# Tile 32's turn inside the pipelined rows, its next gather ahead of its scatter, and the closing norm's arguments on GpSimd

## What is computed

```
x  = x + gt1 * y
h2 = rms_norm(x) * (1 + sc2) + sh2
g  = top-1 of 4 groups, then the top-2 of its 8 experts, weights = softmax * group probability
y  = sum over the 2 experts of  w_e * ( silu(h2 @ gate_e) * (h2 @ up_e) ) @ down_e      # 1024 -> 128 -> 1024
out = rms_norm(x + gt2 * y, final_g)
```

## Time and profile before

| | us |
|---|---|
| median of 3 runs (lowest, highest) | 945.08 (943.24, 945.47) |
| the profiled execution's own time | 939.78 |
| its span in the profile | 938.0 |
| TensorE (matmul) busy | 874.8 (93%) |
| VectorE, GpSimd, ScalarE busy | 457.0, 277.3, 253.6 |
| granted TensorE clock, mean | 0.978 |

### The profile page before, as it was taken

How to read it: one execution, slowest core, us unless ns; L and a number is a source line. 1 busy time by engine, 2 the same in 40 slices (tenths; PEclk the granted TensorE clock), 3 DMA queues, 4 the chain that set the end, 5 groups by cost and what they waited for, 6 DMA issues and landing times. The chain is left out here.

```text
span 938.0 us, 17412 instructions
## 1 busy us (share of the span) xinstructions
PE 874.8 (93%) x7182; PEld 597.2 (64%) x7182; DVE 457.0 (49%) x1140; ACT 253.6 (27%) x608; POOL 277.3 (30%) x264
## 2 busy tenths in 40 slices
PE   5989999999999999999999899999999999999950
PEld 5554445565544447888887745555688888888830
DVE  4820477666731104565665324434464555555534
ACT  5320122222300102545444311221313223222203
POOL 4810000000399400524235010000023566544232
PEclk9999999999999999999999999999999999999995
DMA  9833433444101104000004037111299999998739
GB/s 343 251 94 98 152 112 112 132 148 161 29 22 46 45 1 180 3 3 3 3 3 157 5 144 304 46 78 57 101 339 313 306 305 278 276 275 252 219 57 358
DMA packets 79493, 136.33 MB, mean 145 GB/s; under 512 B 16989, under 2 KB 51002, under 8 KB 79418
## 3 DMA queue, kind: packets, MB, share of 16 engines
q1 hardware_dynamic: 69258, 118.44, 36.4%
q0 software_dynamic: 10160, 16.82, 7.5%
HBM read 123.65 MB, written 29.92 MB: 164 GB/s over the span
## 5 line engine op out<-in xcount | busy, mean ns | idle before, releaser
L752 PE MATMUL bank<-REG_W 128*128 128x512 f32 (+1 forms) x864 | 281.6, 508 | 6.5 <-DVE REG_P L1684 2.5
L752 PEld LDWEIGHTS bank<-REG_W 128*128 128x128 f32 (+1 forms) x864 | 123.3, 176 | 149.4 <-issue 144.5
L752 PE MATMUL bank<-REG_W,REG_Y 128*128 128x512 f32 x256 | 118.3, 599 | 1.4 <-DVE REG_Y L2036 1.1
L1295 ACT ACTIVATE REG_P<-bank 128x256 f32<-128x256 f32 (+2 forms) x126 | 56.9, 460 | 183.8 <-PE bank L752 149.5
L752 PE MATMUL bank<-REG_P 64*64 64x64 f32 (+1 forms) x2816 | 86.8, 222 | 7.2 <-issue 3.3
L752 PEld LDWEIGHTS bank<-REG_P 64*64 64x64 f32 x2816 | 81.1, 135 | 12.4 <-issue 5.8
L752 PEld LDWEIGHTS bank<-REG_W,REG_Y 128*128 128x128 f32 x256 | 45.6, 191 | 44.3 <-issue 44.2
L1295 ACT ACTIVATE REG_Y<-bank,mod,s 128x128 f32<-128x128 f32 x132 | 49.6, 456 | 86.5 <-PE bank L1248 86.5
L752 PEld LDWEIGHTS bank<-REG_Y,REG_W 128*128 128x128 f32 (+1 forms) x640 | 65.7, 181 | 8.4 <-issue 8.4
L752 PE MATMUL bank<-REG_Y,REG_W 128*128 128x128 f32 (+1 forms) x640 | 69.0, 276 | 2.1 <-DVE REG_Y L1905 2.1
L609 POOL TENSOR_TENSOR REG_P<-REG_P 128x1040 f32<-128x1040 f32 x2 | 4.8, 2391 | 194.8 <-DVE REG_P L1635 194.7
(11 more groups left out here) (286 smaller groups left out, 1190.9 us busy)
## 6 DMA issues: line engine op xcount, KB each, us to landing
REG_P<-in_w_ada SPq DMA_DIRECT2D x18, 1024.0 KB, 6.2
REG_W<-in_w_in SPq DMA_DIRECT2D x17, 512.0 KB
REG_P<-in_moe_w_gate SPq DMA_DIRECT2D x17, 512.0 KB, 8.3
REG_W<-in_moe_w_gate SPq DMA_DIRECT2D x16, 512.0 KB, 6.2
REG_W<-in_moe_w_up SPq DMA_DIRECT2D x16, 512.0 KB, 9.5
REG_W<-in_moe_w_down SPq DMA_DIRECT2D x16, 512.0 KB, 14.4
REG_P<-in_moe_w_up SPq DMA_DIRECT2D x14, 512.0 KB, 14.5
REG_P<-in_w_ada SPq DMA_DIRECT2D x3, 2048.0 KB, 12.1
```

The costliest lines, as they stand in the source:

```text
L752: return pe.matmul(o_, l, r, start=start, stop=stop, skip_group_check=True)
L1295: return act.activation(o_, i_, f, **kw)
```

## The change

- TensorE, ScalarE, VectorE: the condition `e + 1 < E` goes, so row 31 also transposes and modulates tile 32. In the overflow loop the transposes and the modulation move to the end of the turn and are those of the next tile (33 in the one turn here). TensorE's transposes then wait for the gather of their tile in the new places.
- GpSimd: `n_ov` is read ahead of the waits for the scatters; in the loop the next tile's gather and the signal `ov_go` stand ahead of the wait for this tile's scatter, the gather ahead of the scatter itself.
- The closing norm goes in the groups (0,1), (2,3), (4,5), (6), (7); GpSimd adds the epsilon and takes the root; VectorE only multiplies; the last tile is multiplied and written in two halves of 512 columns.

```diff
+FINAL = ((0, 1), (2, 3), (4, 5), (6,), (7,))
@@ SP
-            for j in range(NT):
+            for j in range(NT - 1):
                 sp.wait_ge(s["f_o"], j + 1)
                 sp.dma_start(outd[j * P:(j + 1) * P, :], x1[:, j]).then_inc(s_fo, 16)
+            for h in range(2):
+                sp.wait_ge(s["f_o"], NT + h)
+                sp.dma_start(outd[(NT - 1) * P:, h * 512:(h + 1) * 512], x1[:, NT - 1, h * 512:(h + 1) * 512]).then_inc(s_fo, 16)
@@ GpSimd
+            n_ov = gp.value_load(idy[0:1, 0:1], min_val=1, max_val=OVT)
             for b in range(RES):
                 gp.wait_ge(s_sc[b], 16 * len(range(b, E, RES)))
-            n_ov = gp.value_load(idy[0:1, 0:1], min_val=1, max_val=OVT)
             with gp.Fori(0, n_ov) as i:
+                gp.wait_ge(s["m_tx"], i + (E + 1))
+                gather(i + (E + 1), 0)
                 scatter_add(rows_of(i + E, 1, i + (E + 1)), 0)
+                gp.sem_inc(s["ov_go"], 1)
                 gp.wait_ge(s_sc[0], i * 16 + 16 * (len(range(0, E, RES)) + 1))
-                gather(i + (E + 1), 0)
-                gp.sem_inc(s["ov_go"], 1)
             gp.sem_inc(s["f_go"], 1)
-            for i in range(NT // 2):
+            for i, tiles in enumerate(FINAL):
+                at = slice(tiles[0], tiles[-1] + 1)
+                gp.wait_ge(s["ss_ready"], 2 * NT + tiles[-1] + 1)
+                gp.tensor_scalar(ss[:, 2, at], ss[:, 2, at], EPS, None, ALU.add).then_inc(s["f_ss"], 1)
                 gp.wait_ge(s["f_ss"], i + 1)
-                gp.tensor_tensor(rs[:, 2, at], ss[:, 2, at], mhalf[:, 0:2], ALU.pow).then_inc(s["rstd_ready"], 1)
+                gp.tensor_tensor(rs[:, 2, at], ss[:, 2, at], mhalf[:, 0:len(tiles)], ALU.pow).then_inc(s["rstd_ready"], 1)
@@ TensorE (ScalarE and VectorE in the same way)
             for e in range(1, E):
-                if e + 1 < E:
-                    ex_t(e + 1, (e + 1) % BUF, 16 * ((e + 1) // BUF + 1))
+                ex_t(e + 1, (e + 1) % BUF, 16 * ((e + 1) // BUF + 1))
                 ex_gu(e, e % 2, e % RING, ...)
                 ex_dn(e - 1, (e - 1) % 2, (e - 1) % RING, wait_free=e >= 3)
...
             with pe.Fori(0, n_ov) as i:
-                ex_t(i + E, 0, i * 16 + 16 * (E // BUF + 1))
                 ex_gu(i + E, 0, 0, "m_", s["ov_w"], i * 48 + 48, False)
                 pe.wait_ge(s["m_yd"], i + E)
                 ex_dn(i + E, 0, 0, "m_", False)
+                ex_t(i + (E + 1), 0, i * 16 + 16 * (E // BUF + 2))
@@ VectorE
-            root_args(0)
-            for i in range(NT // 2):
-                if i + 1 < NT // 2:
-                    root_args(i + 1)
+            for i, tiles in enumerate(FINAL):
                 dve.wait_ge(s["rstd_ready"], 2 * NT + i + 1)
-                for j in (2 * i, 2 * i + 1):
-                    stt(x1[:, j], x1[:, j], rs[:, 2, j:j + 1], fg, ALU.mult, ALU.mult).then_inc(s["f_o"], 1)
+                for j in tiles:
+                    wide = D if j < NT - 1 else D // 2
+                    for c0 in range(0, D, wide):
+                        stt(x1[:, j, c0:c0 + wide], x1[:, j, c0:c0 + wide], rs[:, 2, j:j + 1], fg[:, c0:c0 + wide],
+                            ALU.mult, ALU.mult).then_inc(s["f_o"], 1)
```

More of the change, by code:

```diff
@@ L520, in _ @@
                 sp.dma_start(x1[:, j], y_d[j * P:(j + 1) * P, :]).then_inc(s_w[j], 16)
-            for j in range(NT):
+            for j in range(NT - 1):
                 sp.wait_ge(s["f_o"], j + 1)
                 sp.dma_start(outd[j * P:(j + 1) * P, :], x1[:, j]).then_inc(s_fo, 16)
-            sp.wait_ge(s_fo, 16 * NT)
+            for h in range(2):
+                sp.wait_ge(s["f_o"], NT + h)
+                sp.dma_start(outd[(NT - 1) * P:, h * 512:(h + 1) * 512], x1[:, NT - 1, h * 512:(h + 1) * 512]).then_inc(s_fo, 16)
+            sp.wait_ge(s_fo, 16 * (NT + 1))
         @block.gpsimd
@@ L731, in _ @@
                     gp.sem_inc(s["ov_go"], 1)
+            n_ov = gp.value_load(idy[0:1, 0:1], min_val=1, max_val=OVT)
             for b in range(RES):
                 gp.wait_ge(s_sc[b], 16 * len(range(b, E, RES)))
-            n_ov = gp.value_load(idy[0:1, 0:1], min_val=1, max_val=OVT)
             with gp.Fori(0, n_ov) as i:
                 ch.enter(i, 4)
+                gp.wait_ge(s["m_tx"], i + (E + 1))
+                gather(i + (E + 1), 0)
                 scatter_add(rows_of(i + E, 1, i + (E + 1)), 0)
+                gp.sem_inc(s["ov_go"], 1)
                 gp.wait_ge(s_sc[0], i * 16 + 16 * (len(range(0, E, RES)) + 1))
-                gather(i + (E + 1), 0)
-                gp.sem_inc(s["ov_go"], 1)
             gp.sem_inc(s["f_go"], 1)
-            for i in range(NT // 2):
+            for i, tiles in enumerate(FINAL):
+                at = slice(tiles[0], tiles[-1] + 1)
+                gp.wait_ge(s["ss_ready"], 2 * NT + tiles[-1] + 1)
+                gp.tensor_scalar(ss[:, 2, at], ss[:, 2, at], EPS, None, ALU.add).then_inc(s["f_ss"], 1)
                 gp.wait_ge(s["f_ss"], i + 1)
-                at = slice(2 * i, 2 * i + 2)
-                gp.tensor_tensor(rs[:, 2, at], ss[:, 2, at], mhalf[:, 0:2], ALU.pow).then_inc(s["rstd_ready"], 1)
+                gp.tensor_tensor(rs[:, 2, at], ss[:, 2, at], mhalf[:, 0:len(tiles)], ALU.pow).then_inc(s["rstd_ready"], 1)
         @block.tensor
@@ L1532, in _ @@
             for e in range(E):
-                if e + 1 < E:
-                    modulated(xt[:, (e + 1) % 2], 0, e + 2, "m_tx", "m_xa", 0)
+                modulated(xt[:, (e + 1) % 2], 0, e + 2, "m_tx", "m_xa", 0)
                 hidden(e, e % 2, free=e >= 2)
@@ L1538, in _ @@
             with act.Fori(0, n_ov) as i:
-                modulated(xt[:, 0], 0, i + (E + 1), "m_tx", "m_xa", 0)
                 hidden(i + E, 0, free=False)
+                modulated(xt[:, 0], 0, i + (E + 2), "m_tx", "m_xa", 0)
             for j in range(NT):
@@ L2049, in _ @@
             for e in range(E):
-                if e + 1 < E:
-                    modulated(xt[:, (e + 1) % 2], e + 2, "m_tx", "m_xd", 1)
+                modulated(xt[:, (e + 1) % 2], e + 2, "m_tx", "m_xd", 1)
                 hidden(e, e % 2, free=e >= 2)
@@ L2061, in _ @@
                 ch.enter(i, 1)
-                modulated(xt[:, 0], i + (E + 1), "m_tx", "m_xd", 1)
                 hidden(i + E, 0, free=False)
-                dve.wait_ge(s_sc[0], 16 * len(range(0, E, RES)))
+                dve.wait_ge(s_sc[0], i * 16 + 16 * len(range(0, E, RES)))
                 result(i + E, 0)
+                modulated(xt[:, 0], i + (E + 2), "m_tx", "m_xd", 1)
             dve.wait_ge(s["xr_ld"], 16 * (NT + 1))
[L2069 to L2072, removed]
-            root_args(0)
-            for i in range(NT // 2):
-                if i + 1 < NT // 2:
-                    root_args(i + 1)
-                dve.wait_ge(s["rstd_ready"], 2 * NT + i + 1)
-                for j in (2 * i, 2 * i + 1):
-                    stt(x1[:, j], x1[:, j], rs[:, 2, j:j + 1], fg, ALU.mult, ALU.mult).then_inc(s["f_o"], 1)
+            for i, tiles in enumerate(FINAL):
+                dve.wait_ge(s["rstd_ready"], 2 * NT + i + 1)
+                for j in tiles:
[3 more added lines that the diff above has]
+                            ALU.mult, ALU.mult).then_inc(s["f_o"], 1)
 _INS = ["x", "c", "w_ada", "b_ada", "norm1_g", "norm2_g", "w_in", "w_out", "pool_w", "pool_scale", "attn_sinks", "conv_w",
```

## The result

The changed kernel takes 954.99 us (median of 6, 950.66 to 957.18) against 944.0 us before (6 runs, 940.47 to 945.47): ratio 1.0115, interval 1.0085 to 1.0145, slower by some 11 us. Forecast was +8.2 us, range +3.4 to +12.4.

A forecast was written before the change was run, and what follows sets the result against it. It took TensorE's row before 897 us, GpSimd's hand-overs to 914.44 and the 23.56 us tail as bounds. Terms +6.9 + 1.7 + 0.3 − 0.7 + 0 = +8.2 us took the 945.08 us median to 953.3, range 948.5 to 957.5.

The forecast's parts named there:

- The gather of tile 32 stops row 31: TensorE, row 31: transposes wait for a gather landing 8.0 us after issue, so gate/up starts at 896.9, not 889.94: +6.9 us.
- The clock: TensorE after its 5.7 us stop: granted clock halves for 3.4 us of work, +1.7 us, bounds 0 and 3.4.
- (a): Rival: TensorE stops at the gather but the clock stays at 2.4 GHz; +6.5 us, 951.6 us; chance 0.18.
- My row at 898: TensorE's 2.09 us gap before the overflow tile's matmuls: a short gap without a clock fall, said not to contradict the rule.
- GpSimd's hand-overs: GpSimd around the overflow tile's scatter: +0.3 us from turn 31's landing to that scatter, −0.7 us from its landing to SP's read.
- The tail: Closing norm from the first read of y_d to the end: 0 us since transfers bound it, bounds −0.6 and +1.2.
- my own last sign: Forecast is wrong if the tail from the first read of y_d differs from 23.56 us by more than 1.5 us.
- the lock: Closing norm: VectorE and GpSimd share a port pair, the loser waiting a whole instruction; VectorE's end +1.2 us, without it −2.2.
- (b): Rival: the tail also pays, +1.2 for GpSimd against VectorE and +1.0 for a delaying gather; 955.5 us; chance 0.16.
- the gather's delay: Tile 33's gather, ahead in the same queue, delays the overflow tile's scatter or the squares: charged nothing, bound +1.0 us.
- (c): Rival: tile 32's gather is there when TensorE asks, so no stop or clock loss; +0.2 us, 945.3 us; chance 0.11.
- (d): Overflow tile: pipelining gains nothing itself, its early data waiting for GpSimd; at most 1.4 us if paid in full; no separate chance.

The follow-up runs named there:

- warm22: The changed kernel with 22 extra matmul calls of unused result ahead of row 31's transposes, so TensorE works through most of its stop: ratio 1.0082 to the kernel before.
- rows_only: The changed kernel with the closing norm of the kernel before; pipelined row and GpSimd's new order stay: ratios 1.0047 and, timed again, 1.0061 to the kernel before.
- tail_only: The kernel before with only the closing norm changed, all of the change's tail: ratio 1.0033 to the kernel before.
- args_pool: The kernel before with the closing norm's arguments on GpSimd, in the four old pairs and with a whole last tile: ratio 1.0027 to the kernel before.
- order_only: The kernel before with GpSimd's new order in the overflow loop alone: ratio 0.9990 to the kernel before.
- ahead_root: The changed kernel with tile 32 gathered earlier, tile 33's gather ahead of the scatter waits, old norm with halved last tile, last pair's roots on ScalarE and VectorE: 942.38 us against 945.8.
- gather_early: The changed kernel with the overflow table loaded behind turn 26 and tile 32 gathered in GpSimd's turn 25 instead of 28: ratio 1.0031 to the kernel before.

## Why the prediction was right, and where not

- **The gather of tile 32 stops row 31, +6.9.** Right in place, cause and size: it lands 8.00 us after its issue, the idle time is 5.46 (5.7 forecast), it goes with an earlier gather (first stretch −8.1, the clock's part included) and grows with a later one. Counted without the clock, in warm22, the first stretch is 19.92 against 13.33: +6.6.
- **The clock, +1.7.** It fell as forecast. It was low for 6.8 us, and TensorE was at work for 5.0 us of them here (forecast 3.4), for 4.4, 3.6 and 3.6 in the other three profiles with the stop. The price by warm22 is 2.34 us here and 2.1 and 1.7 in the kernel of rows_only: the term was at the low end, and one execution's row couldn't size it. The fall at 70 us that I took it from lasts 3.4 us in nine of the 14 profiles and 6.8 in five. Rival (a), no fall, is out: the fall stands in all four profiles with a stop that TensorE idled through. My row at 898, the gap of 2.09 us that had no fall, was luck: in tail_only and args_pool the clock falls after that same gap of the old order (2.08 and 2.09 us), gate/up of turn 32 takes 5.35 and 5.46 us instead of 3.83, and tile 32's scatter comes 1.6 us later.
The Trainium skill (TensorE: Matmul & The Clock Gate, "Why this matters for your kernels") warns of the half clock after an idle gap between bursts of matmuls; the trace agrees (0.50 from 899.7 to 906.5).
- **GpSimd's hand-overs, +0.3 − 0.7.** Sum −1.05 measured in the changed kernel, −0.1 in order_only. From turn 31's landing (920.41) to the scatter of tile 32 it is 2.93 us, where I had 3.5 (before 3.28): the first index copy starts 0.39 us after the landing and not 0.8, and the second follows the gather at once. That the early data of tile 32 would buy nothing, since GpSimd stands at its two index copies, is nearly so in this order (0.5 us), but it is no property of the early data: in ahead_root they allow 2.25 us less than before, more than the 1.4 us that I gave as the most.
- **The tail, 0.** This is the step that failed: "Neither decides", since the transfers are the bound. The step-by-step for VectorE was right (+1.2 forecast, +1.1 here), and in this profile transfers hid most of it: the last write landed 0.4 us later. Over the profiles they did not: the last write is counted 24.0 us after the first read on average with the new tail and 23.0 with the old. Above all I ended the sum with the last write. GpSimd's DRAIN, which stands in the profile of before in the view of the program's last line, ended level with it, and the new tail moved it past the write. The term is +2.4 in this pair of profiles, of which 2.0 behind the last write; by the means of six and four profiles it is +2.9 (26.1 against 23.3), of which 1.8 behind it. By my own last sign (a tail that differs from 23.56 us by more than 1.5) this part of the forecast is wrong; that the sum still came near is due to the size of the stop.
The Trainium skill (SBUF — State Buffer, "SBUF: two separate sides") gives the lock that holds GpSimd's argument beside a multiply; the trace agrees (0.24 us beside an idle VectorE; 0.67 to 1.32 beside one at work, where the argument ends just behind a multiply's end: 940.37 behind 940.2).
- **Rivals.** (b), the tail also pays, is what happened, at +10.2 us in the stretches and +10.9 by the ratio, against its +10.4. Of its mechanism the lock (+1.2) is there; the gather's delay (+1.0) is 0.4 at most (tile 32's scatter lands after 4.73 us, before 4.36), and what stands in its place is GpSimd's DRAIN. That its number is met is luck. (c), the gather being there in time, is gather_early, where the order pays off no more than forecast. (d) held for this order of GpSimd, but for 0.5 us.

Not tried: the changed kernel with its last root taken off GpSimd and nothing else, which would show the DRAIN's part alone; and scattering tile 32 without waiting for turn 31's scatter to land, which would take away the longest wait left (6.5 us), since both may add to the same rows of y_d.

## What to carry to other kernels

When a step moves up in an engine's list, its wait moves with it and blocks all that stands behind: read the issue and the landing of what it waits for, and move that first. A look at the last writer is not a look at the end: compare also when each engine's closing DRAIN ends, and see whether a last small operation on GpSimd can go to another engine. And compare two single profiles from a point behind the last clock fall that the change can't have caused, and don't size a term of the clock from one execution.

## What the runs showed that I had not expected

- GpSimd's closing DRAIN ended 6.9 to 7.0 us after its last operation in all 14 profiles, with a root of one column or two.
- The granted clock falls in stretches where TensorE hardly idles (77 of 80 us busy between 430 and 510 us), in some executions and not in others (1.00 in the profile of before, 0.87 in that of the changed kernel): the executions of the kernel before spread from 940 to 956 us.
- The gap of 2.09 us ahead of turn 32's gate/up was followed by a clock fall in two of the six profiles with the old order.
- Behind a scatter issued 1.85 us earlier, the gather of tile 32 took 8.0 us to land with weights in flight, and 4.7 with the weights nearly through. The gather of tile 33, all of whose rows are skipped, took 4.8 us beside SP's read-back in the kernel before and 2.2 ahead of it in the changed one (921.61 to 923.86).
